# Attention scores of a head pair on the two row halves, with four score banks and three job banks

## The reference

```python
h = layer_norm(concat(meta, x))
qa, ka, va, ga, qi, ki, wi, cq, ckv, kpe, gb = split(h @ w_in)
# sparse branch, 8 heads of 64: indexer picks the keys
rel = einsum('bqhd,bkd->bqhk', qi, ki) / 8
idx_score = einsum('bqhk,bqh->bqk', relu(rel), wi)        # causal, meta tokens always
sel = top_k(idx_score, 128)
la = qa . ka[sel] / 8 + rel_bias[t5_bucket(t - sel)];  oa = softmax(la) @ va[sel]
# dense branch, 8 heads, 64 nope and 32 rope columns, latent q and k/v
q_nope, q_pe = split(rms_norm(cq) @ w_uq);  k_nope, vb = split(rms_norm(ckv) @ w_ukv)
lb = (q_nope . k_nope + rope(q_pe) . rope(kpe)) * 96 ** -0.5;  ob = softmax(causal(lb)) @ vb
mixed = concat(oa * silu(ga), ob * silu(gb))
out = layer_norm(ALPHA * h + mixed @ w_out)
```

## Time and profile before

| what | value |
|---|---|
| time, median of 3 runs | 359.71 us (359.68 to 360.07) |
| the profiled execution | 358.49 us |
| its span | 356.6 us |
| PE busy | 333.8 us, 94% |
| DVE, ACT, POOL busy | 230.1, 171.4, 160.9 us |
| mean granted clock | 0.994 |

### The profile page before, as it was taken

The page is one execution under the profiler, slowest core; times in us unless marked ns, Lnnn a source line. Parts: engine busy times, 40 slices in busy tenths (PEclk is TensorE's granted clock), DMA queues, the critical chain, the costliest instruction groups (busy, mean ns, idle before and its releaser), DMA issues.

```text
span 356.6 us, 6190 instructions
## 1 busy us (share of the span) xinstructions
PE 333.8 (94%) x2187; PEld 275.0 (77%) x2187; DVE 230.1 (65%) x618; ACT 171.4 (48%) x378; POOL 160.9 (45%) x140
## 2 busy tenths in 40 slices
PE   1899999999999899999999999999999999999990
PEld 1588887877888669786868887887888797997980
DVE  6762310299775989897976785448767755534666
ACT  4764633442553335547443644763776643612230
POOL 4432999686251613455303470743234231630563
PEclk9999999999999999999999999999999999999997
DMA  7373333249211222112100140531313230140033
GB/s 281 149 239 134 131 99 112 80 162 302 75 59 59 73 106 56 34 59 80 58 15 2 59 149 2 142 97 34 107 43 89 91 89 3 59 120 2 0 119 119
DMA packets 11566, 32.87 MB, mean 92 GB/s; under 512 B 2392, under 2 KB 2392, under 8 KB 11536
## 3 DMA queue, kind: packets, MB, share of 16 engines
q1 hardware_dynamic: 8944, 27.08, 22.7%
q10 hardware_dynamic: 2592, 5.40, 5.3%
HBM read 29.83 MB, written 4.81 MB: 97 GB/s over the span
## 4 chain that ended last, share of the span: by engine, by line
PE 85%; DVE 8%; issue 3%; ACT 2%; DMA 1%; DVEq 0%; SPq 0%; ACTq 0%
PE ps_j L1176 54%; PE ps_o L1420 6%; PE ps_s L1369 5%; PE ps_s L1377 3%; PE ps_j L1218 2%; PE ps_t L1390 2%; PE ps_s L1337 2%; PE ps_t L1395 1%; PE ps_s L1379 1%; DVE iw L1007 1%; PE ps_j L1229 1%; PE ps_j L1234 1%; DMA res<-in_x 1%; DVE tmp L983 1%; PE ps_t L1399 1%
## 5 line engine op out<-in xcount | busy, mean ns | idle before, releaser
L514 POOL TENSOR_TENSOR wl<-raw,wh 128x1024 fp32r<-128x1024 f32 (+2 forms) x33 | 77.2, 2348 | 93.4 <-ACT wh L521 93.3
L1176 PE MATMUL ps_j<-hh,wh 128*128 128x512 f32 (+2 forms) x224 | 80.1, 358 | 1.5 <-ACT v_b L724 1.4
L1176 PE MATMUL ps_j<-hl,wh 128*128 128x512 f32 (+2 forms) x224 | 77.9, 348 | 0.0
L1176 PE MATMUL ps_j<-hh,wl 128*128 128x512 f32 (+2 forms) x224 | 77.7, 347 | 0.0
L644 POOL TENSOR_SCALAR pr<-pr,rden 128x528 f32<-128x528 f32 (+1 forms) x64 | 34.2, 552 | 54.2 <-DVE rden L1065 54.2
L1176 PEld LDWEIGHTS ps_j<-hh,wh 128*128 128x128 f32 (+1 forms) x224 | 41.9, 187 | 11.9 <-issue 4.2
L1176 PEld LDWEIGHTS ps_j<-hh,wl 128*128 128x128 f32 (+1 forms) x224 | 41.8, 187 | 5.5
L1176 PEld LDWEIGHTS ps_j<-hl,wh 128*128 128x128 f32 (+1 forms) x224 | 41.8, 187 | 5.5 <-issue 0.2
L521 ACT ACTIVATE wh<-raw 128x1024 fp32r<-128x1024 f32 (+2 forms) x35 | 35.9, 1040 | 2.9 <-DMA raw<-in_weights 2.9
L1176 PE MATMUL ps_j<-wh,hh 128*128 128x256 f32 (+1 forms) x112 | 32.1, 286 | 1.1 <-DVE res L976 1.1
L1176 PE MATMUL ps_j<-wl,hh 128*128 128x256 f32 (+1 forms) x112 | 31.4, 280 | 0.0
(11 more groups left out here) (225 smaller groups left out, 758.4 us busy)
## 6 DMA issues: line engine op xcount, KB each, us to landing
raw<-in_weights SPq DMA_DIRECT2D x37, 512.0 KB, 3.4
bias_by_distance<-bias_vector ACTq DMA_DIRECT2D x1, 2624.0 KB, 13.7
bias<-bias_by_distance ACTq DMA_DIRECT2D x8, 264.0 KB, 2.7
res<-in_x SPq DMA_DIRECT2D x4, 512.0 KB, 4.7
out<-res SPq DMA_DIRECT2D x3, 512.0 KB, 2.6
pt<-in_ln_emb_g SPq DMA_DIRECT2D x1, 512.0 KB, 5.5
pt<-in_ln_emb_b SPq DMA_DIRECT2D x1, 512.0 KB, 6.8
q_b<-qpe ACTq DMA_DIRECT2D x8, 64.0 KB, 2.0
```

Of the source, the lines that this page charges most:

```text
L514: eng.tensor_tensor(ring_of(False, b), raw_of(b), ring_of(True, b).bitcast(F32), ALU.subtract).then_inc(done, 1)
L1176: last = pe.matmul(dst, a, b, start=n == 0 and part[0], stop=n == count - 1 and part[1])
```

## The change

**Scores.** A stage is now `S(p, part)` for the pair p of heads, part 0 for tiles 3, 1, 0, part 1 for tile 2. `ps_s` has four banks, two for each head (1,024 columns apart), and `ps_t` is gone. Dense scores are made of one pass over 96 stacked rope rows per head (`kr`, `qr`: high, low, high parts against high, high, low), the causal addition, and three passes over the nope part with both heads at once, on the row halves (`qb`, `kb`). Sparse scores are made of a mask product for each piece group (512, 432 and 400 columns) and the same three passes. The rope rows go to DRAM (`ROPEH` on ScalarE, `ROPEL` on VectorE, and their DMAs on ScalarE's queue) and come back as `ROWS(p)`, 384 KB for a pair.

**Banks.** `ps_j` has three banks, `BANK` and `PRIOR` say which, and `bank_free` waits for the job before in the same bank. The transposes of a head are the jobs `t1` (emptied by ScalarE), `t2` (VectorE) and `t3` (ScalarE, two copies). `PV` is one stage. Evictions of `qn`, `kn`, `qa` and `ka` are one ScalarE copy of 128 rows and one VectorE operation that depends on it.

**Indexer.** Tile 1 of the two heads goes one after the other into the halves of `ps_o`, the second after `i_first`; ScalarE has five ReLUs for a pair instead of six.

**Order.** `schedule()` is rewritten for pairs (in the diff: the new lines; those that they replace are in the code above).

```diff
-SOFF = [800, 0, 1024, 272]
+SOFF = [800, 0, 0, 272]
+MOFF = [800, 0, 944, 272]
 UNITS = [[3, 1, 0], [2]]
+PIECES = [[[(1, 0, 272), (3, 0, 240)], [(3, 240, 528), (0, 0, 144)]], [[(2, 0, 400)]]]
 CO = [0, 512, 912, 1184, 1328]
 IOFF = [896, 1024, 512, 0]
...
+    order.append(("ROPEL", 0))
     job("qpe", 1)
-    pick(2)
+    order.append(("ROPEH", 1))
+    pick(1)
+    order.append(("ROPEL", 1))
+    pick(1)
     job("gate", 6)
-    need(BLOCKS[0], 2)
     pick(5)
     job("uv", 0, 0, extra=0)
     job("uv", 0, 1, extra=0)
+    need(BLOCKS[0], 2)
     job("gate", 7, extra=0)
     job("uv", 0, 2, extra=0)
     job("uv", 0, 3, extra=0)
@@ -188,69 +197,92 @@
     job("kn", 0, 0, extra=0)
     job("kn", 0, 1, extra=0)
     job("uv", 0, 4, extra=0)
-    order.append(("QPE", 0))
+    order.append(("ROWS", 0))
     pick(3)
     job("va", 0, 0)
...
+    def transposes(g):
+
+        for kind in ("t1", "t2", "t3"):
+            order.append(("J", kind, g, 0))
+
+    def first_part(p):
+
+        a, b = 2 * p, 2 * p + 1
+        order.extend([("S", p, 0), ("N", a, 0), ("X", a, 0)])
+        if p:
+            transposes(a - 1)
+        order.extend([("N", b, 0), ("X", b, 0), ("R", a, 0)])
+
+    def second_part(p):
+
+        a, b = 2 * p, 2 * p + 1
+        order.extend([("S", p, 1), ("N", a, 1), ("X", a, 1), ("N", b, 1), ("X", b, 1), ("R", a, 1), ("R", b, 1)])
+
...
```

```diff
+    for p in range(PAIRS):
+        first_part(p)
...
+        job("va", *va.pop(0), extra=0)
...
+            order.append(("PV", p - 1))
+        second_part(p)
...
+            job("qn", p + 1, extra=0)
+            order.append(("ROWS", p + 1))
+            pick(1)
+            job("kn", p + 1, 0, extra=0)
+            job("kn", p + 1, 1, extra=0)
+            job("va", *va.pop(0), extra=0)
+            pick(1)
...
+        transposes(2 * p)
```

```diff
+    job("ka", 0, 0, extra=0)
+    job("ka", 0, 1)
+    for p in range(PAIRS, 2 * PAIRS):
+        q = p - PAIRS
+        first_part(p)
+        if q + 1 < PAIRS:
+            job("qa", q + 1, extra=0)
+        else:
+            for _ in range(3):
+                job("out", *outs.pop(0))
+        order.append(("R", 2 * p + 1, 0))
+        order.append(("PV", p - 1))
+        second_part(p)
...
+        if q + 1 < PAIRS:
+            job("ka", q + 1, 0, extra=0)
+            job("ka", q + 1, 1, extra=0)
+            transposes(2 * p)
+            need(BLOCKS[0], 2)
+    order.extend([("MIX", 0), ("MIX", 1)])
+    for _ in range(5):
         job("out", *outs.pop(0))
-    order += [("TP", 2 * HEADS - 1), ("J", "tq", 2 * HEADS - 1, 0), ("MIX", 2)]
+    transposes(2 * HEADS - 2)
+    order.append(("MIX", 2))
+    for _ in range(4):
+        job("out", *outs.pop(0))
+    transposes(2 * HEADS - 1)
     while outs:
         job("out", *outs.pop(0))
-    order += [("PV", HEADS - 1, 0), ("PV", HEADS - 1, 1)]
+    order.append(("PV", HEADS - 1))
...
+         "qn": (1, 1), "kn": (1, 1), "va": (1, 0), "qa": (1, 1), "ka": (1, 1), "out": (0, 1), "t1": (1, 0), "t2": (0, 1),
+         "t3": (2, 0)}
...
+BANK = [j if j < 2 else (j - 2) % 3 for j in range(len(JOBS))]
+PRIOR = [max([i for i in range(j) if BANK[i] == BANK[j]], default=None) for j in range(len(JOBS))]
...
+            def bank_free(j):
+
+                if PRIOR[j] is not None:
+                    pe.wait_ge(job_act, BY_ACT[PRIOR[j] + 1])
+                    if BY_DVE[PRIOR[j] + 1]:
+                        pe.wait_ge(job_dve, BY_DVE[PRIOR[j] + 1])
+                elif BANK[j] == 2:
+
+                    pe.wait_ge(vec_cp, 2)
...
+                    if part:
+                        pe.wait_ge(e_done if p < PAIRS else s_min, 8 * p + 5)
+                    elif p:
+                        pe.wait_ge(e_done if p <= PAIRS else s_min, 8 * p)
+                    for pieces in PIECES[part]:
+                        for e in range(2):
+                            if p < PAIRS:
+                                for n, (i, a, b) in enumerate(pieces):
+                                    s = 1024 * e + SOFF[i]
+                                    pe.matmul(ps_s[:, s + a:s + b], qr[:, e, i * P:(i + 1) * P], kr[:, a:b], start=n == 0,
+                                              stop=False, skip_group_check=True)
+                                for i, a, b in pieces:
+                                    s, c0 = 1024 * e + SOFF[i], NK[i] - 144
+                                    lo = max(a, c0)
...
+                                        pe.matmul(ps_s[:, s + lo:s + b], identb[:, :], causal[:, lo - c0:b - c0],
+                                                  start=False, stop=False, skip_group_check=True)
+                            else:
+                                (i, a, _), (j, _, b) = pieces[0], pieces[-1]
+                                s = 1024 * e
+                                pe.matmul(ps_s[:, s + SOFF[i] + a:s + SOFF[j] + b], identb[:, :],
+                                          mask[:, MOFF[i] + a:MOFF[j] + b], start=True, stop=False, skip_group_check=True)
+                    qx, kx = (qb[:, :, :], kb[:, :, :]) if p < PAIRS else (qs[:, q % 2, :, :], ks[:, q % 2, :, :])
+                    for pieces in PIECES[part]:
+                        for i, a, b in pieces:
+                            for n, (x, y) in enumerate(((0, 0), (1, 0), (0, 1))):
+                                for e in range(2):
+                                    r, s = slice(HD * e, HD * e + HD), 1024 * e + SOFF[i]
+                                    last = pe.matmul(ps_s[:, s + a:s + b], qx[r, x, i * P:(i + 1) * P], kx[r, y, a:b],
+                                                     start=False, stop=n == 2, skip_group_check=True)
+                    last.then_inc(s_mm, 1)
...
```

More of the change, by code:

```diff
@@ L285 @@
 LAST_JOB = [NJ[last_reader(_b)] for _b in range(len(BLOCKS))]
-LAST_IN_JOB = max(n for n, j in enumerate(JOBS) if j[0] not in ("out", "tq"))
+LAST_IN_JOB = max(n for n, j in enumerate(JOBS) if j[0] not in ("out", "t1", "t2", "t3"))
 TOPK_HALF = [(3,), (0, 1, 2)]
@@ L344, in build @@
         with ExitStack() as latent:
-            k_b = sb("k_b", [96, 2, T], into=latent)
-            q_b = sb("q_b", [96, 2, NQ], into=latent)
+            with ExitStack() as scratch:
+                kpe = sb("kpe", [96, 2, T], into=scratch)
+            kb = sb("kb", [P, 2, T], F32R, latent)
+            qb = sb("qb", [P, 2, NQ], F32R, latent)
+            kr = sb("kr", [3 * ROPE, T], F32R, latent)
             cqh = sb("cqh", [P, 2, NQ], F32R, latent)
@@ L828, in _ @@
+                    if part == 0 and HEADS <= g < 2 * HEADS - 2:
+                        spread_bias(g - HEADS + 2)
                 elif stage == "MIX":
@@ L1416, in _ @@
-                    for j, (t0, r) in list(enumerate(CHUNKS))[1 if part else 0:None if part else 1]:
+                    if n == 0:
+                        pe.wait_ge(wi_cp, 1)
+                        pe.wait_ge(job_act, BY_ACT[NJ["uv", 0, 4] + 1])
+                    else:
+                        pe.wait_ge(o_mix, n)
+                    if n == PAIRS:
+                        pe.wait_ge(job_act, BY_ACT[NJ["va", 1, 4] + 1])
+                    pe.wait_ge(job_act, BY_ACT[NJ["t3", 2 * n + 1, 0] + 1])
```

552 lines of the change are left out of this document (250 added, 302 removed).

## The result

The changed kernel takes 402.24 us (median, 401.88 to 402.88), the kernel before 359.89 (359.68 to 360.2): the ratio is 1.1178, 95% interval 1.1158 to 1.1197. It is slower by 42.4 us, where 22.7 were forecast and 392 was the upper end of the range. The profiled execution has a span of 401.0 us, against 356.6.

A forecast was written before the change was run, and what follows sets the result against it. TensorE was taken to set the time, with products saved and new waits counting whole. Seven terms summed to +22.7 us on the median of 359.71, giving 382.4 us; own range 374 to 391, bounds with varied waits 366 and 392.

The forecast's parts named there:

- 1 dense scores: Dense score products on TensorE: a head pair takes 4.72 us instead of 5.44, saving 2.9 us over four pairs.
- 2 sparse scores: Sparse score products on TensorE: a head pair takes 4.04 us instead of 3.98, costing 0.2 us.
- 3 indexer: Indexer: tile 1 of two heads no longer together, second group waits for all four additions; costs 1.8 us.
- 4 stretch to the first dense scores: From 119 to 136 us: 3.0 us of losses go, 4.5 of new waits come; costs 1.5 us.
- 5 bank of `qn`: Pairs 0 to 2: `va` waits for VectorE to empty `qn`, 2.4, 3.2 and 2.4 us; costs 7.0 net.
- 6 bank of the transposes: First parts 1 to 7: the next job waits for ScalarE's copy behind three exps; seven waits cost 14.8 us.
- 7 PV: The rest: unsplit PV -1.3, first sparse scores and head 6 transposes +1.6, late `out0,3` bank +1.3, end projection -1.3 us.
- the clock falls: Rival: after each of ten waits the next job runs at 1.2 GHz, 20 us more, 403 us; chance 0.05.
- The halves do not run together: Rival: row-half products writing one `ps_s` tile step one after another, about 399 us; chance 0.03.
- Only one hold: Rival: only one of the waits at the `qn` bank and the transposes' bank bites, about 373 us; chance 0.12.
- Neither hold bites: Rival: no new wait at the `qn` or transposes' bank, so the kernel gets faster, 351.3 us; chance 0.09.

The follow-up runs named there:

- e11_fewer_picks: Changed kernel with transposes, `va`, `mix`, rope and pick stages reordered, lastly two picks moved from ahead of the first dense scores into pairs 0 and 3; 359.05 us, 0.9995.
- e4: Changed kernel with products nobody reads run into `ps_o` where TensorE waited behind transposes and ahead of `va` jobs; 391.7 us.
- e6: Changed kernel with the high and low parts of two sparse `mix` chunks made later, one behind each of the next transposes; 394.1 us.
- e3_both: Changed kernel with the edits of e1 and e2 together; 377.3 us.
- e1: Changed kernel with the stages of the three transposes moved ahead of the minima and exps of the new scores; 381.5 us.
- e7: Changed kernel with the first rope rows' low part made ahead of the last indexer stage and the second rope rows behind gate 6; 399.1 us.
- e2: Changed kernel with the picks around the eviction of `qn` put behind the evictions of `qn` and `kn`; 397.8 us.
- e5: Kernel of e1 with a `va` job between `qn` and the `kn` jobs, the weight cast and three picks behind the `kn` jobs; 375.3 us.

## Why the prediction was wrong

The sum named the places rightly and left out one consequence. By its own steps, in us, from the two profiled executions:

| term | forecast | measured |
|---|---|---|
| 1 dense scores | -2.9 | -2.4 |
| 2 sparse scores | +0.2 | -1.9 |
| 3 indexer | +1.8 | +2.2 |
| 4 stretch to the first dense scores, without the clock | +1.5 | +2.6 |
| 5 bank of `qn` | +7.0 | +6.8 |
| 6 bank of the transposes | +14.8 | +15.3 |
| 7 PV; first `ka`; `out1,2` bank; end | -1.3, +1.6, +1.3, -1.3 | -0.8, +2.1, +5.0, -1.8 |
| the lower clock (estimate) | 0 | +15.4 |
| opening, ahead of the indexer | 0 | +1.5 |

The measured column adds to 44.0; the spans differ by 44.4. Terms 1 to 7 alone are 27.1, which on the median of before is 387, within the forecast's own range. The opening is no term of the change: the indexer started at 63.6 us here, at 61.6 in e11_fewer_picks, with the same code ahead of it.

**The step that failed** is the term of the clock: the sum put it at nothing, and the runs showed 15.4 us. The mechanism "the clock falls" was written down with its price, 20 us more, and given 0.05, on the ground that no wait of such length stands between products in the trace of before. That is a reason for not knowing, and I used it as one against. What I had named from the Trainium skill stood beside it ("would make this case" went further than that section, whose gaps are longer than these waits), and the trace of before had nothing that spoke against it: its waits after the opening are all under 2 us. Its opening even has slow products, after 7.75 us in which TensorE had done nothing and nine more with pauses:

```profile
16.49 1.20 PE L1229 MATMUL ps_j<-hh,wh 128*128 128x512 f32 x2
17.49 0.86 PE L1234 MATMUL ps_j<-hh,wl 128*128 128x512 f32 x2
```

Two products of 512 columns take 1.00 us from start to start there, 0.50 each, against the 0.23 of the later rows. The granted clock reads 1.00 for that stretch, so that it was the lower one is inferred from the times. A sum that puts ten waits of 2 to 3 us into a stream that had none should have carried the clock in its likeliest case. (The chances as written, with "no change" counted apart, add up to 1.02.) Its size was over-estimated in turn: 15.4 us are 10.6 (six dips, by e4), 2.3 (by e6) and some 2.5 for the one from 125.2 to 132.0 us, an estimate from the granted clock (0.50, with TensorE busy 5.4 of the 6.8 us). The trace agrees: in the eight stretches TensorE was busy for 30.4 us at 0.50, and half of that is 15.2. Ten waits gave six dips of 1.6 to 1.8 us and not ten of 2. That the rival's 403 lies within 1 us of the measured time is luck: its clock was 4.6 too dear, and what the sum left out or mis-sized elsewhere makes up for it.

**Term 7, `out1,2`** was mis-sized: 2.2 for the wait, measured 5.9. I took the low parts of `mix` at 0.69 each; they took 2.64. Rows of before showed it: L1090 in the sparse section took 2.48 us at 245.62 and at 267.10 and 0.68 at 255.98, and I didn't ask why.

**Term 2** was wrong in sign: a sparse pair takes 3.46 us (3.68 in e11_fewer_picks) and not 4.04; before, the mean was 3.94. I priced the mask products and the two round trips at 2.0 us together, too dear; I have not separated the two. **Term 3** was right: a pair takes 2.44 and 2.50, later 2.86 and 2.84, where the second group waits for all four additions; 2.10 to 2.12 before. **Terms 5 and 6**, 21.8 forecast, are 22.1. The single `qn` waits were 2.9, 2.8 and 2.1 against 2.4, 3.2 and 2.4. **Term 4** has the waits for `uv` (2.5), gate 7 (1.8), `va0,0` and `ROWS` (1.0 and 0.9) in the places named: the first two larger than the 0.75 and 1.1 forecast, the others smaller than or near the 1.7 and 1.0.

**The rivals.** "The halves do not run together" fell by the trace: the two products of a pair start 2 to 6 ns apart. "Only one hold" fell, since both have their forecast size. "Neither hold bites" fell, and its 351 us fell too: with most of the waits removed the best order reached 359.05, not 351. The profile of that kernel, e11_fewer_picks, still has 1.1 + 0.9 + 0.8 + 0.8 + 0.8 us of waits around the first two dense pairs. From the first dense to the first sparse scores it takes 85.1 us, as the kernel before does: its score products are 2.1 us shorter there, and its transposes 1.3, its jobs 0.6 and its products with the values 0.5 us longer, short waits counted in. Why they are longer, and the rest of the difference, I have not traced.

**Not settled:** which waits bring the clock down. In the changed kernel that of 2.9 us at 157 us did not, the next, of 2.4 us at 169 us, did; those of 2.4, 2.0 and 2.1 us at 196, 277 and 325 us did not. In idle time the shortest that was followed by a dip is 1.83 us (e3_both, at 155 us) and the longest that was not is 2.7 (the one at 157 us, and the same in e1, e6 and e7). The same wait can go either way: that of 2.3 us for the `uv` weights is followed by a dip in the changed kernel and in e1, e2, e4 and e6, and not in e3 and e5, which have the same order up to there. So part of what each edit above gained or lost is chance, some 1.7 us a dip. e2_picks_behind, whose executions lie 5.6 us apart, fits three dips more or less, but only one execution has a trace. Pauses of up to 1.4 us, the 1.44 of the earlier trace rows among them, never did here.

## What to carry to other kernels

When stages are put in a new order, follow each bank from its last write to its next, and list what stands ahead of the emptying copy in the queue of the engine that makes it; seven groups of exps in the way cost 15 us here, and moving three stages gave it back. Where a sum puts new waits of 2 us or more into a busy TensorE, let its likeliest case carry the clock too: here six of ten such waits cost another 1.6 to 1.8 us. Products that nobody reads are a quick test of which part is wait and which is clock. The scores themselves saved 4.3 us and the indexer took 2.2 of it back; this change was decided by its order, not by its products.
